# The first attention's scores as two fp32r products of stacked high and low parts, with the pair's columns ordered q, k, v, gate

## The reference

```python
h = rmsnorm(x, norm_g[i])
p = h @ fox_w_in[j]
W = FOX_WIDTH
q = p[..., :W].reshape(B, S, FOX_HEADS, FOX_HEAD_DIM)
k = p[..., W:2 * W].reshape(B, S, FOX_HEADS, FOX_HEAD_DIM)
v = p[..., 2 * W:3 * W].reshape(B, S, FOX_HEADS, FOX_HEAD_DIM)
gate = p[..., 3 * W:4 * W]
log_f = jax.nn.log_sigmoid(p[..., 4 * W:].astype(jnp.float32) + fox_b_f[j].astype(jnp.float32))
...
    s = jnp.einsum('bqhd,bkhd->bhqk', qi.astype(jnp.float32), kf) * scale
    s = s + ci[..., None] - c[:, :, None, :]
    ...
    s = jnp.where(mask[None, None], s, NEG_INF)
    p = jax.nn.softmax(s, axis=-1).astype(v.dtype)
    return jnp.einsum('bhqk,bkhd->bqhd', p, v)
...
y = y * jax.nn.silu(gate)
x = x + y @ w_out
```

## Time and profile before

| | us |
|---|---|
| median of 3 runs | 3231.86 |
| lowest and highest | 3221.24, 3236.97 |
| the profiled execution | 3234.71 |
| its span | 3232.9 |

### The profile page before, as it was taken

How to read it: one execution, slowest core, us unless ns; L and a number is a source line. 1 busy time by engine, 2 the same in 40 slices (tenths; PEclk the granted TensorE clock), 3 DMA queues, 4 the chain that set the end, 5 groups by cost and what they waited for, 6 DMA issues and landing times.

```text
span 3232.9 us, 39162 instructions
## 1 busy us (share of the span) xinstructions
PE 3079.9 (95%) x15418; PEld 2439.5 (75%) x15418; DVE 1673.4 (52%) x2844; ACT 1185.3 (37%) x2070; POOL 230.5 (7%) x437
## 2 busy tenths in 40 slices
PE   8999999999999999999999989999999998988897
PEld 6777777777768887777778868787787877867786
DVE  5444444444443336566553354756566555465546
ACT  4333333333323324344333333444444343434413
POOL 0000000000000000000000001202012020203002
PEclk9999999999999999999999999999999999999999
DMA  4222222222224322222234322212223121214444
GB/s 160 77 79 72 79 77 77 76 79 72 79 82 146 117 92 66 66 71 66 66 115 138 118 79 80 80 59 80 79 67 90 56 87 54 81 57 136 139 131 150
DMA packets 84980, 288.89 MB, mean 89 GB/s; under 512 B 11056, under 2 KB 11696, under 8 KB 84544
## 3 DMA queue, kind: packets, MB, share of 16 engines
q1 hardware_dynamic: 67680, 239.99, 23.4%
q0 software_dynamic: 17120, 46.41, 4.5%
HBM read 261.13 MB, written 25.17 MB: 89 GB/s over the span
## 4 chain that ended last, share of the span: by engine, by line
PE 79%; DVE 11%; ACT 4%; issue 2%; DMA 2%; POOL 1%; SPq 0%; DVEq 0%; ACTq 0%; POOLq 0%
PE bank L261 14%; PE bank L263 13%; PE bank L262 13%; PE bank L265 7%; PE bank L267 7%; PE bank L266 7%; PE bank L285 2%; PE bank L1294 2%; ACT mc_split L538 1%; PE bank L1230 1%; PE bank L1225 1%; DVE mc_split L694 1%; PE bank L314 1%; PE bank L449 1%; PE bank L294 1%
## 5 line engine op out<-in xcount | busy, mean ns | idle before, releaser
L261 PE MATMUL bank<-ma_split,mc_split 128*128 128x512 f32 x2304 | 962.9, 418 | 23.7 <-DVE ma_split L837 10.3
L694 DVE TENSOR_TENSOR mc_split<-mc,mc_split 128x1024 fp32r<-128x1024 f32 x434 | 533.6, 1230 | 860.9 <-ACT mc_split L538 859.3
L263 PE MATMUL bank<-ma_split,mc_split 128*128 128x512 f32 x2304 | 909.2, 395 | 0.0
L262 PE MATMUL bank<-ma_split,mc_split 128*128 128x512 f32 x2304 | 906.5, 393 | 0.0
L538 ACT ACTIVATE mc_split<-mc 128x1024 fp32r<-128x1024 f32 x434 | 459.5, 1059 | 911.4 <-PE bank L261 512.1
L261 PEld LDWEIGHTS bank<-ma_split,mc_split 128*128 128x128 f32 x2304 | 438.9, 191 | 144.1 <-issue 50.0
L263 PEld LDWEIGHTS bank<-ma_split,mc_split 128*128 128x128 f32 x2304 | 437.3, 190 | 97.6
L262 PEld LDWEIGHTS bank<-ma_split,mc_split 128*128 128x128 f32 x2304 | 439.7, 191 | 78.3 <-issue 4.1
L265 PE MATMUL bank<-mc_split,ma_split 128*128 128x512 f32 x576 | 230.6, 400 | 0.7 <-DVE mc_split L694 0.3
L267 PE MATMUL bank<-mc_split,ma_split 128*128 128x512 f32 x576 | 225.5, 391 | 0.0
L266 PE MATMUL bank<-mc_split,ma_split 128*128 128x512 f32 x576 | 225.2, 391 | 0.0
(11 more groups left out here) (359 smaller groups left out, 3625.3 us busy)
## 6 DMA issues: line engine op xcount, KB each, us to landing
mc<-in_w SPq DMA_DIRECT2D x434, 512.0 KB, 3.6
x<-mc POOLq DMA_DIRECT2D x8, 1024.0 KB, 5.3
ma_split<-y POOLq DMA_DIRECT2D x28, 256.0 KB, 4.3
mb<-in_xt SPq DMA_DIRECT2D x8, 512.0 KB, 9.8
mc<-in_x POOLq DMA_DIRECT2D x4, 1024.0 KB, 6.0
mc<-x POOLq DMA_DIRECT2D x4, 1024.0 KB, 7.2
mats<-mc POOLq DMA_DIRECT2D x32, 128.0 KB, 2.6
mc<-inv POOLq DMA_DIRECT2D x8, 512.0 KB, 5.3
```

The costliest lines, as they stand in the source:

```text
L261: mm = pe.matmul(banks[j][:], wh[:, c], act_hi[:, kt, :], start=(kt == 0), stop=False)
L262: pe.matmul(banks[j][:], wl[:, c], act_hi[:, kt, :], start=False, stop=False)
L263: last = pe.matmul(banks[j][:], wh[:, c], act_lo[:, kt, :], start=False, stop=(kt == KT - 1))
L694: dve.tensor_tensor(w_low[:, s % NR, :, :], w_raw[:, s % NR, :, :], w_high[:, s % NH, :, :].bitcast(F32), ALU.subtract).then_inc(w_lo, 1)
```

## The change

**Operands.** Head `e` gets two pairs of operands in fp32r. `q_both` holds q's high part on the head's own 64 rows and its low part on the other 64; `k_twice` holds k's high part on both. `q_ones` holds q's high part on the head's rows and ones on two of the others; `k_sums` holds k's low part on the head's rows and, on those two rows, the high and the low part of the sum of the forget gate. The first product is then high by high plus low by high, the second is high by low plus the sums. A unit's scores are these two products, over max(keys, 256) columns, and the mask as before.

**Who makes them.** `fox_take` takes q and k out whole, with 128 rows in one instruction each, into `q_raw32` and `k_raw32`. From these, ScalarE writes the high parts of `q_ones` and `k_twice` (`fox_high`, four instructions), GpSimd the high parts of `q_both` and the other half of `k_twice` (four casts), and VectorE the low parts (`fox_low`, four subtractions). The forget gate's sums are split too, by one copy on ScalarE and one subtraction on VectorE, once; GpSimd then does four row transfers a pair.

**Order.** The pair's columns are now q, k, v, gate in banks 0 to 3. The first unit's scores move from the fourth tile of the block to the end of the first slot (point 7). `fox_high` and `fox_low` stand in slot 0 ahead of that slot's weight split. `k_raw32` lies in the area beyond the buffers of x, `q_raw32` in the first exponentials' buffer, and `q_both` and `k_twice` share the space of `xb[0]`, so the first load of x moves from the start to behind the last pair's scores.

```diff
@@ fox_scores
                 if k == 0:
-                    pe.wait_ge(bank_free[2], FOX0 + c + 1)
-                    pe.wait_ge(bank_free[3], FOX0 + c + 1)
-                    pe.wait_ge(fc_in, 32 * (c + 1))
+                    pe.wait_ge(qk_hi, 4 * c + 4)
+                    pe.wait_ge(qk_lo, 4 * c + 4)
+                    pe.wait_ge(qk_copied, 4 * c + 4)
+                    pe.wait_ge(fc_in, 64 * (c + 1))
                 if n >= 2:
                     pe.wait_ge(p_exp, n - 1)
-                pe.matmul(bank[:, 0:nk], qz[:, e, b * P:(b + 1) * P], kz[:, e, 0:nk], start=True, stop=False)
+
+                w = max(nk, 2 * P)
+                pe.matmul(bank[:, 0:w], q_both[:, e, b * P:(b + 1) * P], k_twice[:, e, 0:w], start=True, stop=False)
+                pe.matmul(bank[:, 0:w], q_ones[:, e, b * P:(b + 1) * P], k_sums[:, e, 0:w], start=False, stop=False)
@@ first_pe
+                        if point == 7 and b <= OUT0:
+                            fox_pe_side(pe, b, s, (b - 1,))
                         if point % 8 != 3:
                             continue
                         if b <= OUT0 + 1:
-                            fox_pe_side(pe, b, s)
+                            fox_pe_side(pe, b, s, (b - 2, b - 1) if s else (b - 2,))
@@ ScalarE
+            def fox_high(act, c):
+
+                for raw, to, taken in ((q_raw32, q_ones, bank_free[0]), (k_raw32, k_twice, bank_free[1])):
+                    act.wait_ge(taken, FOX0 + c + 1)
+                    for e in range(2):
+                        hs = slice(e * HD, (e + 1) * HD)
+                        act.activation(to[hs, e, :], raw[hs, :], ACT.Copy).then_inc(qk_hi, 1)
...
+                        if 1 <= b <= OUT0 and s == 0:
+                            fox_high(act, b - 1)
                         split_act(act, BLOCK_SLOTS * b + s + LEAD)
...
+                            act.wait_ge(fc_ready, 1)
+                            act.activation(f_c[0:HEADS, :], f0[0:HEADS, :], ACT.Copy).then_inc(f_log, 1)
@@ fox_take
                 if c:
-                    dve.wait_ge(v_turned, c)
-                dve.tensor_tensor(v_raw, banks[0][:], rb, ALU.mult).then_inc(bank_free[0], 1)
+                    dve.wait_ge(s_done, 8 * c)
+                    dve.wait_ge(t_done, 8 * c - 1)
+                dve.scalar_tensor_tensor(q_raw32, banks[0][:], 0.125, rb, ALU.mult, ALU.mult).then_inc(bank_free[0], 1)
                 dve.wait_ge(gemm_done, 4 * c + 2)
-                dve.tensor_tensor(gate2[:, c % 2, :], banks[1][:], rb, ALU.mult).then_inc(bank_free[1], 1)
+                dve.tensor_tensor(k_raw32, banks[1][:], rb, ALU.mult).then_inc(bank_free[1], 1)
                 dve.wait_ge(gemm_done, 4 * c + 3)
                 if c:
-                    dve.wait_ge(s_done, 8 * c)
-                st(dve.tensor_tensor(kz[0:HD, 0, :], banks[2][0:HD, :], rb[0:HD, :], ALU.mult))
-                dve.tensor_tensor(kz[HD:P, 1, :], banks[2][HD:P, :], rb[HD:P, :], ALU.mult).then_inc(bank_free[2], 1)
+                    dve.wait_ge(v_turned, c)
+                dve.tensor_tensor(v_raw, banks[2][:], rb, ALU.mult).then_inc(bank_free[2], 1)
                 dve.wait_ge(gemm_done, 4 * c + 4)
-                st(dve.scalar_tensor_tensor(qz[0:HD, 0, :], banks[3][0:HD, :], 0.125, rb[0:HD, :], ALU.mult, ALU.mult))
-                dve.scalar_tensor_tensor(qz[HD:P, 1, :], banks[3][HD:P, :], 0.125, rb[HD:P, :], ALU.mult, ALU.mult
-                                         ).then_inc(bank_free[3], 1)
+                dve.tensor_tensor(gate2[:, c % 2, :], banks[3][:], rb, ALU.mult).then_inc(bank_free[3], 1)
+
+            def fox_low(dve, c):
+
+                for i, (raw, high, to) in enumerate(((q_raw32, q_ones, q_both), (k_raw32, k_twice, k_sums))):
+                    for e in range(2):
+                        hs = slice(e * HD, (e + 1) * HD)
+                        at = slice((1 - e) * HD, (2 - e) * HD) if to is q_both else hs
+                        dve.wait_ge(qk_hi, 4 * c + 2 * i + e + 1)
+                        dve.tensor_tensor(to[at, e, :], raw[hs, :], high[hs, e, :].bitcast(F32), ALU.subtract).then_inc(qk_lo, 1)
@@ first_dve
+                        if 1 <= b <= OUT0 and s == 0:
+                            fox_low(dve, b - 1)
                         split_dve(dve, BLOCK_SLOTS * b + s + LEAD)
@@ first_pool
-                pool.dma_start(xb[0], x_rows[:, :, 0:N]).then_inc(res_in[0], 16)
-                pool.wait_ge(fc_ready, 1)
+                pool.wait_ge(fc_ready, 2)
                 for c in range(PAIRS):
                     if c:
                         pool.wait_ge(s_done, 8 * c)
-                    pool.dma_start(kz[HD:HD + 1, 0, :], f_c[2 * c:2 * c + 1, :]).then_inc(fc_in, 16)
-                    pool.dma_start(kz[0:1, 1, :], f_c[2 * c + 1:2 * c + 2, :]).then_inc(fc_in, 16)
+                    for e in range(2):
+                        for i in range(2):
+                            row, frm = (1 - e) * HD + i, HEADS * i + 2 * c + e
+                            pool.dma_start(k_sums[row:row + 1, e, :], f_c[frm:frm + 1, :]).then_inc(fc_in, 16)
+
+                    for raw, to, taken in ((q_raw32, q_both, bank_free[0]), (k_raw32, k_twice, bank_free[1])):
+                        pool.wait_ge(taken, FOX0 + c + 1)
+                        for e in range(2):
+                            hs = slice(e * HD, (e + 1) * HD)
+                            at = slice((1 - e) * HD, (2 - e) * HD) if to is k_twice else hs
+                            pool.tensor_copy(to[at, e, :], raw[hs, :]).then_inc(qk_copied, 1)
+                pool.wait_ge(s_done, 8 * PAIRS)
+                pool.dma_start(xb[0], x_rows[:, :, 0:N]).then_inc(res_in[0], 16)
@@ host
-    pair = [fw[:, j * D:(j + 1) * D].reshape(D, PAIRS, 1, P) for j in (2, 3, 1, 0)]
+    pair = [fw[:, j * D:(j + 1) * D].reshape(D, PAIRS, 1, P) for j in range(4)]
```

## The result

The changed kernel took 3188.07 us (median of four, 3182.31 to 3192.64) against 3233.07 us before (median of four): a ratio of 0.9866, with a 95% interval of 0.9834 to 0.9897. It is 45 us faster, 1.3% by the ratio; 3183 was forecast. The profiled execution has a span of 3188.9 us.

The account below looks back on a forecast made before the run. The PE's own stream, busy 95% of the span, was taken as the bound. Scores 28 us plus seam 21 us, operands at nothing, gave 49 us off: 3184 us profiled, 3183 against the median; range 3173 to 3218.

Parts of the forecast that it names:

- the two gains: First attention beside blocks 1 to 16: cheaper scores 28 us and no seam wait 21 us, 49 us together.
- Scores: Score units on the PE: a pair falls from 4.32 to 2.5 us, 29 us over 16 pairs, 28 after waits.
- The upper bound: Score products on the PE: weight loads of 0.19 us that no longer hide would cost 10 us in all.
- four passes: Short fp32r score products at 0.43 us each would turn a pair's gain into a loss of 0.7 us.
- The loss in pairs 0 and 15: Softmax waits there eat what units 2 and 6 save: 0.3 us each, 1.2 us for the two pairs.
- Seam: Start of a block's products: the PE's wait for the takes goes, 1.39 us at 15 seams, 21 us.
- Operands: New work on ScalarE, VectorE, GpSimd and row transfers before a pair's first scores: hidden, half a microsecond of cover.
- the exclusion: VectorE subtractions and GpSimd casts: one stands until the other's instruction ends; takes, which read PSUM, are not affected.
- 352.0 + 4x: End time of a pair's last cast or subtraction, x being one cast: 354.6 at 0.65 us, deadline 355.15.
- third rival: Slower: PE waits over 4 us before each pair's first unit, behind GpSimd casts from 1.8 us; chance 0.08.
- 4x - 3.15: PE wait before each pair's first unit, x being one cast; times 16, 84 us at x = 2.1.
- Moving x's load: First load of x goes into block 16: 19 us of products left against 6.0 us to land, hidden.

Follow-up runs that it names:

- the other kernels that keep it: Kernel before with columns as q, k, v, gate only, 3236.42 us; kernel before with four whole takes but fp32 score products, 3212.07 us.
- with six takes: Changed kernel with v and gate each taken in two halves of 64 rows: 3202.43 us, ratio 0.9914 against the kernel before.
- the run with three casts: Changed kernel with two extra same-size casts into a spare buffer before each of GpSimd's four: 3285.81 us, ratio 1.0165 against the kernel before.

## Why the prediction held

**What bounds, and the two gains.** Right. The PE's stream bounds, and scores and seam are the gains; both were shown apart and they add.

**Scores.** 1.83 us a pair was forecast and 1.62 measured, 26 us in place of 29. Scaling the 512-column product by its width held from the first product of a unit to the second: 0.113 us at 256 columns, 0.171 at 384. Mis-sized was what stands behind: from the second product to the mask pass 0.01 us more than that, the mask takes 0.01 us longer than it did behind the fp32 product, and the first 512-column product behind v's transposes costs 0.32 us in place of 0.23. Over eight units these make the 0.2 us. The upper bound, a weight load of 0.19 us, did not bind. Nor did four passes. The loss in pairs 0 and 15 came as worked out: the waits for the softmax rose from 7.1 to 8.4 us, 1.3 where 1.2 was said.

**Seam.** 1.39 forecast, 1.2 measured, 18 us in place of 21. The mis-sized term is the 4.23 us from tile 0's first product to the transposes: its start, 349.19, is the timeline's, its end, 353.42, the chain's. The timeline before has the transposes 0.16 us earlier:

```profile
353.26 0.60 PE L294 MATMUL bank<-ident,mc 128*128 128x128 f32 x4
```

Taken from one view it is 4.07 us, less twelve steps of 0.2275 us and the 0.08 that stay, 1.26. The step into tile 0 grew by 0.02 us (0.29 to 0.31) on top. The takes of v and gate ended at 335.10 and 335.70, 0.4 and 0.5 us before the PE's products into their banks (0.3 was said for v's), and nothing else came late.

**Operands.** Hidden, as forecast, with 1.16 us in hand and not 0.5. Casts took 0.61 us (0.65 said), subtractions 0.69 alone. Of the exclusion I was half right: only the last of the four casts was slowed, to 0.96 us (the gaps between the casts are 0.06 us each), and the two subtractions beside it took 0.74 and 0.99. The formula, 352.0 + 4x, was too strict; twice the casts showed a wait of 1.5 us where the same rule, worked out from the changed kernel's trace, gives 2.3. The figure of the Trainium skill (GPSIMD Engine Reference, section 3.1, 769 ns for 512 elements) is above the 0.61 us that the casts took; the measurement decides. That the move to the end of the slot is what hides all this is measured too: without it, 27 us are lost.

**The third rival's price.** The mechanism exists and was priced too low. At 8.4 us of casts the kernel is 1.65% slower than before (rival 3's side), where the formula has 35 us slower, 3267, and 3286 was measured. Two steps of its price failed, in opposite directions: the wait was to be 5.25 us by 4x - 3.15 at x = 2.1 and was 4.2, and 16 x wait was too little, since a wait of 4.2 us cost 6.2, the PE's clock falling behind it.

**What was not foreseen.** Moving x's load from the start I costed as hidden where it went, and did not ask what it had hindered where it came from. It held up the weights of block 0: the first take came 4.4 us earlier between the two profiled executions, 4.1 us with the load alone moved, and 0.5 to 2 us by the other kernels that keep it. Against it, block 1 was 0.5 us longer (62.75 to 63.24). Its granted clock from 80 to 120 us was 0.96 against 1.00 before, behind a wait for the softmax in pair 0. Kernels with the same block 1 and no dip had 61.6 us, so this cost 1.6 us in that execution. The length of the wait alone doesn't decide it: with six takes the same wait of 1.91 us (102.41 to 104.33) was followed by no dip, and what does decide it is not shown. The two terms that were too large and the one that was missing partly cancel, and so 3183 is only 5 us from the median; that much of it is luck.

## What to carry to other kernels

A result that is taken out of PSUM by more instructions than there are banks holds up the next block's products even when the engine that does it is half idle; taking whole banks and spreading them later, off the banks' way, gave 1.2 us a block here. Operands that need work by three engines can be free, if the first use is moved by the few products that cover them; read the margin from the timeline (here 1.16 us) and test it by doubling the work. Where a transfer is moved away from a busy stretch, count what it held up there.

## What the runs showed of the hardware

- A GpSimd cast and a VectorE subtraction with two SBUF inputs slow each other (0.61 to 0.95 us and 0.69 to 0.99 us), but pass together in 1.02 us, less than their sum; a cast and a take from PSUM don't slow each other (0.61 and 0.68 us).
- A GpSimd cast of 64 x 512 that shifts by 64 rows took as long as one that doesn't, 0.61 us (in the run with three casts, at 312.46 and 314.48, where VectorE had finished).
- An fp32r product of 128 columns kept its rate up to the next product, 0.06 us; the step from the second one into the bf16 mask stayed at 0.12 us with 128 as with 256 columns.
- An fp32r product directly behind a group of transposes is followed late: after 0.31 us in place of 0.23 for 512 columns, 0.20 in place of 0.11 for 256.
- Behind a halt of the PE of 4.2 us the granted clock was 0.55 in the next 3.4 us; behind halts of 1.5 us it stayed at 1.00. Behind a halt of 1.9 us in block 1 it fell in some executions (0.96 from 80 to 120 us in the changed kernel) and not in others (1.00 with six takes).
